# Three instead of two tiles begin each stage of a hybrid decoder step on their first 256 tokens, with square sums in spare PSUM columns and gated scores by head

## What is computed

```
def trunk(x, pos, s_gla, s_ret, norm_g, w1_gu, w1_down, ...):
    for l in range(DEPTH):                                   # 2
        x = x + 0.5 * rmsnorm(swiglu(rmsnorm(x, n[0]), w1_gu[l], w1_down[l]), n[1])
        m, S_a, S_r = mixer(rmsnorm(x, n[2]), pos, w_in[l], w_a2[l], ..., w_out[l], s_gla[l], s_ret[l])
        x = x + rmsnorm(m, n[3])
        x = x + 0.5 * rmsnorm(swiglu(rmsnorm(x, n[4]), w2_gu[l], w2_down[l]), n[5])

def gla_chunk(S, inp):                                       # gated heads, key dimension 64
    q, k, v, lg = inp
    b = jnp.cumsum(lg, axis=2)
    o_inter = jnp.einsum('bhtk,bhkv->bhtv', q * jnp.exp(b), S)
    diff = b[:, :, :, None, :] - b[:, :, None, :, :]
    decay = jnp.exp(jnp.where(causal_mask()[:, :, None], diff, -jnp.inf))
    A = jnp.einsum('bhtk,bhsk,bhtsk->bhts', q, k, decay)
    ...
```

## Time and profile before

| | |
|---|---|
| median of three runs | 2269.41 us (2269.36 to 2269.57) |
| the profiled execution's own time | 2269.25 us, span 2267.4 us |
| TensorE's mean granted clock in it | 0.998 |

### The profile page before, as it was taken

How to read it: one execution, slowest core, us unless ns; L and a number is a source line. 1 busy time by engine, 2 the same in 40 slices (tenths; PEclk the granted TensorE clock), 3 DMA queues, 4 the chain that set the end, 5 groups by cost and what they waited for, 6 DMA issues and landing times.

```text
span 2267.4 us, 43365 instructions
## 1 busy us (share of the span) xinstructions
PE 2222.5 (98%) x17639; PEld 2191.9 (97%) x17639; DVE 842.3 (37%) x1166; ACT 817.8 (36%) x1429; POOL 947.4 (42%) x776
## 2 busy tenths in 40 slices
PE   8999999999999999999999999999999999999998
PEld 7999999999989999999999999999999889999998
DVE  5222200589366422220152222006883772222102
ACT  4332333442344433332343333334424443333333
POOL 3444444444214444444444444453442334444442
PEclk9999999999999999999999999999999999999999
DMA  6223223322234232223322322332222333232222
GB/s 173 87 84 92 72 85 89 91 76 74 66 82 131 75 92 84 86 74 90 113 67 84 91 83 73 90 100 73 79 72 58 99 112 93 83 89 85 76 85 76
DMA packets 382588, 197.57 MB, mean 87 GB/s; under 512 B 8868, under 2 KB 381400, under 8 KB 382360
## 3 DMA queue, kind: packets, MB, share of 16 engines
q1 hardware_dynamic: 365680, 186.93, 28.8%
q10 hardware_dynamic: 16808, 9.20, 1.4%
HBM read 186.80 MB, written 9.31 MB: 86 GB/s over the span
## 4 chain that ended last, share of the span: by engine, by line
PE 94%; DVE 4%; ACT 1%; issue 1%; DMA 0%; ACTq 0%; DVEq 0%
PE ps L529 87%; PE ps L692 1%; PE ps L850 1%; DVE x L1439 1%; DVE y L1433 0%; DVE y_out L1433 0%; DVE xs_lo L1377 0%; PE ps L667 0%; PE ps L791 0%; PE ps L764 0%; DVE q_lvl L1524 0%; PE ps L867 0%; PE ps L770 0%; PE ps L797 0%; ACT xs_hi L1026 0%
## 5 line engine op out<-in xcount | busy, mean ns | idle before, releaser
L465 POOL TENSOR_TENSOR w_lo<-raw,w_hi 128x512 fp32r<-128x512 f32 (+1 forms) x728 | 914.7, 1261 | 1219.1 <-ACT w_hi L1053 1219.0
L529 PE MATMUL ps<-xs_hi,w_hi 128*128 128x256 f32 (+1 forms) x3712 | 789.0, 290 | 16.9 <-DVE xs_lo L1377 13.5
L529 PE MATMUL ps<-xs_hi,w_lo 128*128 128x256 f32 (+1 forms) x3712 | 786.4, 289 | 0.0
L529 PE MATMUL ps<-xs_lo,w_hi 128*128 128x256 f32 (+1 forms) x3712 | 783.6, 288 | 0.0
L1053 ACT ACTIVATE w_hi<-raw 128x512 fp32r<-128x512 f32 (+1 forms) x728 | 420.1, 585 | 959.9 <-PE ps L529 959.0
L529 PEld LDWEIGHTS ps<-xs_hi,w_hi 128*128 128x128 f32 x3712 | 604.5, 189 | 25.9 <-DVE xs_lo L1377 10.6
L529 PEld LDWEIGHTS ps<-xs_lo,w_hi 128*128 128x128 f32 x3712 | 604.2, 189 | 0.4
L529 PEld LDWEIGHTS ps<-xs_hi,w_lo 128*128 128x128 f32 x3712 | 600.9, 188 | 0.0
L1398 DVE TENSOR_TENSOR tmp<-ps,rstd_pre 128x544 f32<-128x544 f32 x88 | 63.8, 725 | 641.4 <-PE ps L529 628.4
L529 PE MATMUL ps<-h_hi,w_lo 128*128 128x256 f32 x1272 | 267.2, 289 | 0.0
L529 PE MATMUL ps<-h_lo,w_hi 128*128 128x256 f32 x1272 | 266.1, 288 | 0.0
(11 more groups left out here) (197 smaller groups left out, 1751.9 us busy)
## 6 DMA issues: line engine op xcount, KB each, us to landing
raw<-in_w_gu_dram SPq DMA_DIRECT2D x176, 512.0 KB, 3.8
raw<-in_w_in_dram SPq DMA_DIRECT2D x56, 512.0 KB, 3.8
raw<-in_w_down_dram SPq DMA_DIRECT2D x64, 384.0 KB, 3.4
raw<-in_w_down_dram SPq DMA_DIRECT2D x64, 320.0 KB, 3.1
raw<-in_w_out_dram SPq DMA_DIRECT2D x16, 512.0 KB, 3.9
ret_state<-in_state_ret_dram SPq DMA_DIRECT2D x8, 512.0 KB, 6.0
out_dram<-ret_state ACTq DMA_DIRECT2D x8, 512.0 KB, 5.0
x_tok<-in_x_prompt_dram SPq DMA_DIRECT2D x4, 512.0 KB, 6.5
```

The lines of the kernel that those rows point to most:

```text
L465: pool.tensor_tensor(lo, raw[:, u, k0:k0 + n, :], hi.bitcast(F32), ALU.subtract)\
L529: mm = pe.matmul(bank_part(bank, a), w, v[:, kx, TOK[a]], start=(start and n == 0), stop=(stop and n == 2))
```

## The change

1. `first_pair` becomes `first_three`: unit 2 as well is run over `TOK[0]` in the first pass and over `TOK[1]` in the second, behind the pair in each. Its split weights have a place of their own, `w_third`, so its split waits for no slot. ScalarE makes it ahead of the second half's `xs_hi`, where it stood behind all squares.
2. `pre_stats` writes into unused columns of banks 0, 1 and 3 (256, 224 and 64 columns) and stands between the halves of unit 3, in the mixer in the middle of the gate's tile. The waits for `pre_log` on TensorE are gone. The logarithm is three instructions.
3. `q_lvl` loses its zero halves. A level's scores are 16 matmuls, for each head 64 rows and 64 columns of queries, into a bank for each head, where there were 8 with 128 rows and 128 columns. VectorE makes `q_lvl` in one instruction. A memset of `q_lvl` is gone. The two loops of `diagonal_scores` change places.

```diff
-            def first_pair(l, q, g0):
+            def first_three(l, q, g0):
...
+                    for half, k0, n in half_units(KD):
+                        if a == 0:
+                            wait_split(g0, 2, half)
+                        for k in range(n):
+                            mm = products(w_third[:, k0 + k, 0, :], w_third[:, k0 + k, 1, :], xs_hi, xs_lo, k0 + k, 4,
+                                          k0 + k == 0, k0 + k == KD - 1, parts=(a,))
+                        if a == 1:
+                            mm.then_inc(split_used[split_slot(2, half)], 1)
...
-                first_pair(l, 2 * f, g0)
-                unit(g0, 2, KD, xs_hi, xs_lo, 0, 4, True, True)
+                first_three(l, 2 * f, g0)
+                unit(g0, 3, KD, xs_hi, xs_lo, 0, 6, True, True, halves=(0,))
                 pre_stats(l, 2 * f)
-                wait(pe, pre_log, l, 2 * f)
-                unit(g0, 3, KD, xs_hi, xs_lo, 0, 6, True, True)
+                unit(g0, 3, KD, xs_hi, xs_lo, 0, 6, True, True, halves=(1,))
...
-                wait(pe, pre_log, l, 1)
                 for k in range(KD):
+                    if k == KD // 2:
+                        pre_stats(l, 1)
...
                     for hh in range(QT):
-                        at = (c_ % 2 * QT + hh) * CH
-                        mm = pe.matmul(ps[:, 4 + 2 * (n % 2) + c_ // 2, at:at + CH].rearrange("p (a t) -> p a t", a=2),
-                                       k_lvl[:, hh, c_ * CH:(c_ + 1) * CH],
-                                       q_lvl[:, hh, :, c_ * CH // 2:(c_ + 1) * CH // 2], start=True, stop=True)
+                        at = (c_ * QT + hh) * (CH // 2)
+                        for p in range(2):
+                            rows = slice(p * DKG, (p + 1) * DKG)
+                            mm = pe.matmul(ps[:, 4 + 2 * (n % 2) + p, at:at + CH // 2],
+                                           k_lvl[rows, hh, c_ * CH:(c_ + 1) * CH],
+                                           q_lvl[rows, hh, c_ * CH // 2:(c_ + 1) * CH // 2], start=True, stop=True)
...
+                split_high(g, 2, FULL_KT, third=True)
                 for k in range(KD):
                     pre_high(l, q, 1, k)
                     if k % 2:
                         pre_square(l, q, k // 2)
-                for u in (2, 3):
-                    split_high(g, u, FULL_KT)
+                split_high(g, 3, FULL_KT)
...
-                root(rstd_pre[:, :], pair(3), q, pre_log, pre_ready, l)
+                for cols, place in STATS_PLACE:
+                    o = act.activation(rstd_pre[:, cols], place, ACT.Ln, bias=eps, scale=1.0 / D)
+                o.then_inc(pre_log.sem, 1)
+                wait(act, pre_log, l, q)
+                act.activation(rstd_pre[:, :], rstd_pre[:, :], ACT.Exp, scale=-0.5).then_inc(pre_ready.sem, 1)
...
-                    for p in range(2):
-                        rows = slice(p * DKG, (p + 1) * DKG)
-                        o = dve.tensor_tensor(q_lvl[rows, :, p, 0:w // 2].rearrange("p q (n m) -> p q n m", m=m),
-                                              by_block(queries, w, m)[rows, :, :, 1, :],
-                                              by_block(e_buf, w, m)[rows, :, :, 1, :], ALU.mult)
-                    o.then_inc(prod_ready.sem, 1)
+                    dve.tensor_tensor(q_lvl[:, :, 0:w // 2].rearrange("p q (n m) -> p q n m", m=m),
+                                      by_block(queries, w, m)[:, :, :, 1, :],
+                                      by_block(e_buf, w, m)[:, :, :, 1, :], ALU.mult).then_inc(prod_ready.sem, 1)
```

More of the change, by code:

```diff
@@ L373, in wait_x, with weight_place @@
                 eng.wait_ge(x_ready.sem, X0 + (l * 3 + q - 1) * 2 * KP + a * KP + k // 2 + 1)
-        def weight_place(u, half, k0, n, keep):
+        def weight_place(u, half, k0, n, keep, third=False):
+            if third:
+                return w_third[:, k0:k0 + n, 0, :], w_third[:, k0:k0 + n, 1, :]
             if keep:
@@ L458, in _, with group @@
             pool.wait_ge(loaded, LOADS)
-            def group(g, kts, order=UNIT_ORDER, keep=()):
+            def group(g, kts, order=UNIT_ORDER, keep=(), first=False):
                 for i, (u, half) in enumerate(order):
                     _, k0, n = half_units(kts[u])[half]
-                    hi, lo = weight_place(u, half, k0, n, u in keep)
+                    hi, lo = weight_place(u, half, k0, n, u in keep, first and u == 2)
                     pool.wait_ge(hi_split, g * (2 * UNITS) + (i + 1))
@@ L497, in _ @@
                 for f in range(2):
-                    group(l * GROUPS + UP[f], FULL_KT, UNIT_ORDER if l or f else PAIR_ORDER)
+                    group(l * GROUPS + UP[f], FULL_KT, UNIT_ORDER if l or f else PAIR_ORDER, first=True)
                     with pool.Fori(1, UP_GROUPS) as i:
@@ L507, in _ @@
                                            ALU.subtract).then_inc(a_split.sem, 1)
-                        with pool.Fori(0, len(IN_GROUPS)) as i:
+                        group(l * GROUPS + WIN, FULL_KT, first=True)
+                        with pool.Fori(1, len(IN_GROUPS)) as i:
                             group(l * GROUPS + WIN + i, FULL_KT)
@@ L554, in pre_stats @@
                 wait(pe, xsq_step, l, q * KP + KP - 1)
-                for a in range(2):
-                    mm = pe.matmul(bank_part(6, a), ones, x_sq[:, 0, TOK[a]], start=True, stop=True)
+                for cols, place in STATS_PLACE:
+                    mm = pe.matmul(place, ones, x_sq[:, 0, cols], start=True, stop=True)
                 mm.then_inc(pre_sum.sem, 1)
@@ L698, in level_scores @@
                     for hh in range(QT):
-                        mm = pe.matmul(ps[0:TS, 4 + 2 * ((n + 1) % 2), hh * TS:(hh + 1) * TS].rearrange("p (a t) -> p a t", a=2),
-                                       k_lvl[:, hh, TP:T], q_lvl[:, hh, :, TP // 2:HALF], start=True, stop=True)
+                        for p in range(2):
+                            rows = slice(p * DKG, (p + 1) * DKG)
+                            mm = pe.matmul(ps[0:TS, 4 + 2 * ((n + 1) % 2) + p, hh * TS // 2:(hh + 1) * TS // 2],
+                                           k_lvl[rows, hh, TP:T], q_lvl[rows, hh, TP // 2:HALF], start=True, stop=True)
                 mm.then_inc(scores_ready.sem, 1)
@@ L708, in diagonal_scores @@
                 t0, t1, n = (TP, T, TS) if sample else (0, TP, P)
-                for p in range(2):
-                    for hh in range(QT):
+                for hh in range(QT):
+                    for p in range(2):
                         mm = pe.matmul(ps[0:n, 4 + 2 * p + hh, 0:t1 - t0], ones[p * DKG:(p + 1) * DKG, 0:n],
@@ L971, in _ @@
                 ffn(l, 0)
[L973 to L975 removed]
+                first_three(l, 1, l * GROUPS + WIN)
                 gate_tile(l)
@@ L1049, in split_high @@
                     _, k0, n = half_units(kts[u])[half]
-                    if not keep:
+                    if not keep and not third:
                         act.wait_ge(split_used[split_slot(u, half)], 2 * g + (u // 2 + 1))
-                    hi, _ = weight_place(u, half, k0, n, keep)
+                    hi, _ = weight_place(u, half, k0, n, keep, third)
                     act.activation(hi, raw[:, u, k0:k0 + n, :], ACT.Copy).then_inc(hi_split, 1)
@@ L1775, in _ @@
                         dve.memset(a_gla.rearrange("p a c x t -> p (a c x t)"), 0.0)
-                        dve.memset(q_lvl.rearrange("p q a t -> p (q a t)"), 0.0)
                         dve.memset(a_gla_s.rearrange("p a x t -> p (a x t)"), 0.0).then_inc(a_zeroed.sem, 1)
```

20 lines of the change are left out of this document (11 added, 9 removed).

## The result

| | before | after |
|---|---|---|
| median | 2269.59 us (six runs, 2269.36 to 2271.14) | 2286.14 us (six runs, 2285.04 to 2287.08) |
| profiled execution, own time and span | 2269.25, 2267.4 us | 2285.78, 2284.0 us |
| TensorE's mean granted clock in it | 0.998 | 0.994 |

The ratio is 1.0072 (95% interval 1.0059 to 1.0085): the changed kernel is slower, by 16.5 us from median to median. The forecast was 2286.5. Traces are of one execution each, and how often the clock falls differs between executions: three of the changed kernel's six show a mean clock of 0.994 (2285.0 to 2285.8 us), the other three 0.992 or 0.993 (2286.5 to 2287.1 us).

The account below looks back on a forecast made before the run. TensorE, busy for 98% of the span, was taken to bound the kernel. The terms 3.5 + 9.0 + 6.8 − 1.2 − 2.8 + 1.9 = +17.2 us on 2269.25 gave 2286.5 us, with a range from 2270 to 2294.

Parts of the forecast that it names:

- very first stage: First SwiGLU stage, no wait ahead of the sums: half a unit, narrow piece and longer logarithm make it +3.5 us.
- three other SwiGLU stages: Starts of the other three SwiGLU stages: second group starts 3.0 us later each, +9.0 us; bounds +1.7 and +4 each.
- four falls of the clock: Behind new idle time in four SwiGLU stages: clock halves for 3.41 us, costing half of that each, +6.8 us.
- mixer's start, two: Start of the two mixers: sums 1.65 us later, unit 3 waits for the first tile's read; −0.6 each, −1.2 us.
- VectorE's part at the levels: First and seventh levels: q_lvl in one instruction for two shrinks four waits by 0.7 us each, −2.8 us.
- level matmuls: Fourteen levels: 16 pairs at 0.11 us, plus 0.1 per change of rows, +1.9 us; bounds −7.6 and +26.
- The chain of 7 us behind the sums: SwiGLU stage starts: from the sums' end through logarithm, SiLU and weight splits to the second group, 7.0 us.
- The first rival: Stage starts: waits go and none comes, 15.8 us less there and 2.8 at the levels, 2252.6 us; 7%.
- The sums' delay: Three later SwiGLU stages: xs_lo comes 2.3 us late, a 1.3 us wait is left, sums end 2.6 us later.
- the two turns: Second half's residual adds: two GpSimd splits alternate with VectorE by whole instructions, over 1.1 us each, 2.3 taken.
- the bound of the forecast: Clock in four SwiGLU stages: falls last twice as long, costing 13.6 us in place of 6.8.
- the third rival: Level scores at half the price because weight loads overlap more: 9.5 us less, 2277 us; 9%.

Follow-up runs that it names:

- sums_only: Kernel before with sums of squares in unused columns at their old places, three logarithms and no TensorE wait for the logarithm: 2269.08 us, ratio 0.9996.
- sums_ahead: Changed kernel with the sums of squares ahead of unit 3, not between its halves, in the four SwiGLU stages: 2270.36 us, ratio 1.0003.
- split_early: Changed kernel in which ScalarE splits the second group's first unit right behind unit 3, ahead of the logarithm: 2263.04 us, ratio 0.9971.
- fill_idle: Changed kernel with nine matmuls of ones in TensorE's idle time between the sums and unit 3's second half, four SwiGLU stages: 2278.91 us, ratio 1.0042.
- no_pairs: Changed kernel with the loop over the two heads outermost in a level's scores, so matmuls don't alternate between row halves: 2319.52 us in one run.
- three_only: Changed kernel without its third part, scores as before on 128 rows with a zero half: 2286.92 us, ratio 1.0072.
- third_by_vector: split_early with the third unit's low part made by VectorE instead of GpSimd, in all but the very first stage: 2257.06 us, ratio 0.9946.
- scores_only: Kernel before with the change's third part alone, scores by head on 64 rows and q_lvl in one instruction: 2268.98 us, ratio 0.9999.
- more_warm: third_by_vector with ten matmuls of ones for five in the idle time ahead of each layer's third stage: 2255.78 us, ratio 0.9938.

## Why the prediction was right, point by point

The time was forecast at 2286.5 and is 2286.1. That it fits to 0.4 us is partly luck: the terms are off by up to 1.8 us, on both sides. The shifts of TensorE's own steps between the two traces, added up by the terms of the sum (us):

| term | forecast | measured |
|---|---|---|
| very first stage | +3.5 | +3.5 |
| three other SwiGLU stages | +9.0 | +7.2 |
| four falls of the clock | +6.8 | +7.2 |
| mixer's start, two | −1.2 | −1.6 |
| VectorE's part at the levels | −2.8 | −3.7 |
| level matmuls | +1.9 | +3.2 |
| sum | +17.2 | +15.8, and 0.7 behind the last stage |

**The chain of 7 us behind the sums** decided, as forecast, and it is shown and not only argued: sums_only leaves the sums where they are and gets the old wait back in a new place, sums_ahead moves them and the wait follows, split_early cuts the chain and the wait goes. The first rival (2252.6) had named the point, that the chain would have to be 3.0 us. split_early makes it 3.35 and comes out at 2263.0, 10.4 us above the rival; 6.0 of these were the turns of GpSimd, and without them it is 2257.1.

**The sums' delay.** In the second layer's first stage the two turns went as forecast (two of VectorE's adds took 1.85 us each for 0.75, 2.2 us late in all), the wait for `xs_lo` is 1.36 us for 1.3, and the second group came 2.7 us later for 3.0. In the third stages, which the forecast treated like the others, it went another way. GpSimd's instruction began there in the middle of VectorE's adds, which followed one another without a pause, and it ended only 1.1 us behind the last of them, after 3.58 us (the first of the two in this row; the second took 1.5):

```profile
739.01 5.05 POOL L473 TENSOR_TENSOR w_third<-raw,w_third 128x512 fp32r<-128x512 f32 x2 [7.08 <-ACT w_third L1072]
```

```profile
738.70 1.42 DVE L1456 TENSOR_TENSOR y_out<-y_out,acc 128x576 f32<-128x576 f32 x2
740.04 1.42 DVE L1462 TENSOR_TENSOR x<-x,y_out 128x576 f32<-128x576 f32 x2
741.39 2.98 DVE L1400 SCALAR_TENSOR_TENSOR xs_lo<-x,vecs,xs_hi 128x288 fp32r<-128x288 f32 x2
```

VectorE is at its usual 0.7 us there, and it is the weights that are late: TensorE waits 1.3 us for `w_third`, a wait that the forecast didn't have, and the two `xs_lo` instructions pay afterwards. The second group came 2.2 and 2.4 us later, not 3.0. The mis-sized term is this one, by 1.8 us.

Which way it goes is tied to the clock. Of the twelve third stages in which a traced kernel has GpSimd make `w_third`, five have no fall at their start, and in these it went as above (both of the changed kernel, both of fill_idle, the first of no_pairs). Seven have one, and there VectorE's adds are late, as forecast, and no wait for `w_third` is listed. The first layer's third stage in sums_ahead, GpSimd and VectorE:

```profile
734.40 3.12 POOL L473 TENSOR_TENSOR w_third<-raw,w_third 128x512 fp32r<-128x512 f32 x2 [7.67 <-ACT w_third L1071]
```

```profile
733.84 2.53 DVE L1455 TENSOR_TENSOR y_out<-y_out,acc 128x576 f32<-128x576 f32 x2 [0.25 <-ACT acc L1055]
```

What differs beside the clock is the distance of the two: GpSimd's instruction begins 0.56 or 0.57 us behind the first of VectorE's adds in the seven, 0.30 to 0.32 us in the five. Whether this decides was not tried. In three_only, where both third stages have the fall, the second group came 2.5 and 2.6 us later.

**The clock.** Four falls came, where they were forecast, and cost 7.2 us (2.1 us in a first stage, 1.5 in a third, and fill_idle gives 7.2 as well). The size was right by two errors: two of the falls last 6.83 us, the bound of the forecast, but their first 2.1 us lie in idle time. And the two falls at the start of the third stages went, which the forecast didn't foresee. They are in the term of the three stages. Why they went, no run explains (last section), so this part of the fit is luck.

**The mixer's start** was 0.8 us earlier, each time, for 0.6. The wait is for the first tile's read (`qk_a`, 0.6 us), as said.

**Levels.** The two terms are both too small and nearly cancel. At the seventh level the whole wait of 1.1 us went and not 0.7: `q_lvl` is one instruction of 0.72 us for two that took 2.54, and `k_lvl` ahead of it takes 1.29 us for 1.97, since GpSimd does no split beside them any more. The matmuls run at 0.12 us a pair: a level takes 1.93 us, more than the 1.7 to 1.8 given as a sign of being right, but half the price is far off and the third rival is out. By its own numbers that rival was sized wrong: 0.055 us a pair takes 0.86 us off each of 14 levels, 12 us and not 9.5, so 2274.5 and not 2277, and the bound would be −10.1 and not −7.6. A change of the rows in use costs more than the 0.1 us taken: at the second to fifth levels a level takes 1.93 us for 1.78, and the 48 matmuls of 256 and 288 tokens behind it 6.23 for 6.03, together 0.34. The first level has 0.2 us and the two with sample tokens none, so that the 14 have 3.2 us, 0.23 on average, where the forecast has 0.14. The Trainium skill's "TensorEngine Tiling (Array Packing)", section "Key Properties", says that a change of tiling mode drains the engine; these 0.34 us agree in kind, though no run sets the drain apart. Of the up to 2x of its "Theoretical Speedup" 1.7 shows, 32 passes in 1.93 for 3.32 us, but the old form had the same work in 16.

## What to carry over

When a step is moved on the engine that bounds the kernel, measure the chain that hangs on that step's result; if it is already as long as the work beside it, a saved wait only changes its name and a later step costs its full delay. Look for what in this chain the waiting operand doesn't need (here the SiLU's table load and product ahead of a weight split) and take it out of the queue: that was worth 23 us, the change itself cost 16. Work on GpSimd that is free by its own time isn't free beside VectorE.

## What the runs showed of the hardware

- The same 2.5 to 2.6 us of standing still ahead of the third stage brought a fall in some cases and none in others: one in both layers in before, sums_ahead, split_early, third_by_vector and three_only, in neither in after and fill_idle, and in one of the two in scores_only, sums_only and no_pairs. So neither the length of the standing still nor the change of the kernel decides, and what does is not settled here; a forecast should carry both. With 0.36 us no fall came (more_warm), with 4.3 us always (12 of 12 in after, three_only and no_pairs). The falls behind 4.3 us last 3.41 or 6.83 us, and the same stage has either: the very first has 6.83 in after and 3.41 in three_only.
- The clock also fell while TensorE was busy without a gap, with matmuls on one half of the rows at a time: in no_pairs at the fifth and seventh level of the first layer and the fifth of the second, 2.8 to 3.1 us after the level began. In the trace of the changed kernel, with the same matmuls in pairs, it never fell at a level. At most levels of no_pairs it didn't fall either. The falls in the mixers (split_early, 654.8) come 1.9 us behind the end of 1.44 us of standing still, which third_by_vector has too, without a fall.
- GpSimd's and VectorE's adds held each other up by whole instructions, in either direction: two of VectorE's at 1.85 for 0.75 us, or one of GpSimd's at 3.58 for 1.3, in two stages of the same kernel. In the second case it ended 1.1 us behind the last of four adds in a row. Which case came went with the clock at the stage's start, in all twelve third stages traced.
